# Keys scored between the granules of the gates, values between those of the next head, in a decoder layer for one core

## The chip, the cores and the metric

One core of a Trainium2 chip runs the kernel. The time is that of the device in microseconds (us), the median of several executions. All tensors are float32.

## The reference, cut to what matters

One layer serves a prompt of 256 tokens and 8 sequences of 8 new tokens each (320 tokens together), with 2,048 channels. One projection `h @ w_in` gives everything that the mixer needs. Branch A is a gated linear recurrence (HGRN2) with 8 heads, branch B a differential attention with 8 heads of two softmax maps each; for the 8 sequences it attends to 2,048 past tokens in 16 pages of a shared cache.

```python
u = h @ w_in[l]
hq, hf, hi, hgate, dq, dk, dv, g_hg, g_da = jnp.split(u, IN_SPLIT_POINTS, axis=-1)
# A: chunks of 64 tokens, state S per head
A = jnp.where(causal, einsum('bhncd,bhnsd->bhncs', qg, kg), 0.0)
o = A @ v + qg @ S_prev;  S = exp(G_last) * S_prev + dS
o_hg = rms_norm(o, hg_norm_w[l]) * silu(hgate)
# B: past keys and values are pages of cache_k and cache_v
p = softmax(q @ k.T * DA_DH ** -0.5 + t5_bias)      # two maps
o_da = rms_norm((p[:, 0] - lam * p[:, 1]) @ v, da_subln_w[l]) * (1.0 - lam_init)
mixed = (sigmoid(g_hg) * (o_hg @ w_branch_hg) + sigmoid(g_da) * (o_da @ w_branch_da)) @ w_out
```

A norm, a residual and a SwiGLU feed-forward with 5,632 hidden channels follow. The updated states, the keys and the values are outputs too.

## The kernel before, in words

**Granules.** The unit of dense work is a granule, a 512 KB piece of weights (128 partitions x 1,024) that multiplies two of the 16 channel tiles of the input into four output tiles of 320 columns. For accuracy each weight is split: ScalarE (ACT) copies it to a rounded `w_hi` (`round_hi`, L368, in the opening L352), VectorE (DVE) subtracts for `w_lo` (`split_lo`, L345), and TensorE (PE) makes three matmuls (L386 to L388) for each, 24 in a granule. Eight granules make a set of four tiles in PSUM banks 0 to 3. There are four buffers for the split weights, so a split runs at most four granules ahead of PE. DVE reads a set's banks in `read_set` (L429), and the next set's first granule waits for this, bank by bank.

**Rounds.** After an opening of 7 sets the kernel runs 8 rounds (`pe_round`, `act_round`, `vec_round`, `sync_round`, `pool_round`). A round has two halves. In the gate half PE does the 8 granules of a set of merge gates (A0 to A7 in the order of transfers), and after granule q the products of a head, `pe_head(q)`: attention of the prompt and the chunked recurrence. In the second half PE does the 8 granules of the next head's set (D0 to D7), and between them the paged attention of one sequence (`pe_mix`): four quads of keys (`scores`, 16 matmuls L797 for four pages in groups of 32 columns), the new keys' scores (L803), the sums of squares for the norms (L828), the transposes of the exponentials (`pt`, L835), 16 pages of values (L817) and the transposes back (L851). The last round has no next head and so no D granules.

**ACT and DVE** run each in the order of their program: `act_round` and `vec_round` give for each granule q the split first, then the head's and the mix's steps of that q. ACT reads a quad's scores (`g0` to `g3`, L679), makes the exponential `p` (L710), squares and square roots (`sq`, `rt`, L697 to L704), copies (`q`, L688 and L691; `o`, `o_second`). DVE takes maxima (`m0` to `m3`, L735 and L751) and the norms' reciprocals (L758, L765).

**Transfers.** All 512 KB pieces go through a ring of 12 slots in the order of the list `ROUND`: kind A (gates), K (a page of keys), D (next head), V (a page of values). The sync queue (SP) issues them strictly in this order (L673), and before each waits until the piece that held its slot is used: a weight when DVE has split it, a page of keys when its quad is scored, a page of values when its matmuls are done.

```python
ROUND = (items("A", 0, 8) + items("K", 0, 4) + items("D", 0, 1) + items("K", 4, 8) + items("D", 1, 2)
         + items("K", 8, 12) + items("D", 2, 3) + items("K", 12, 16) + items("D", 3, 6) + items("V", 0, 8)
         + items("D", 6, 7) + items("V", 8, 16) + items("D", 7, 8))
```

GpSimd's queue (POOL) stores the gate set, the new states, and then loads the next head's tiles and old states (`head_loads`, L413 to L421).

**Banks.** Banks 4 to 7 serve the head's products and the paged attention in turn: scores alternate between 4 and 5, the head's output `o` is in 5, its new-state product `ds_s` in 6 and 7. `Steps` are the counters by which the engines wait for each other; a name such as `s0` or `g3` is one step of a round.

Of the kernel before, what the change touches and what calls it, by code (L numbers as in the profile page):

```python
# [19 lines left out]
ALU = mybir.AluOpType  # L20
ACT = mybir.ActivationFunctionType
AX_X = mybir.AxisListType.X
F32 = mybir.dt.float32
# [50 lines left out]
def items(kind, a, b):  # L74
# [40 lines left out]
def build(nc, xT, ck, cv, st, pt, w_in, w_hg, w_da, w_out, w_up, w_dn, nrm, hgw, lbl, lamv,  # L115
          table, c_ident, c_scan, c_causal, c_own, c_hot, c_coef,
          y_T, k_T, v_T, h_p, h_s):
    with ExitStack() as ctx:
# [65 lines left out]
        v_new = sb("v_new", [NQ, HEADS * DV], F32, at_r)  # L184
# [10 lines left out]
        state = sb("state", [P, 4, DV], F32, at_r)  # L195

# [3 lines left out]
        lg = sb("lg", [P, T], F32, at_h)  # L200
# [3 lines left out]
        kd = sb("kd", [P, T], F32, at_h)  # L204
# [4 lines left out]
        i_own = sb("i_own", [CHUNK, NB, DV], F32, at_h)  # L209
# [8 lines left out]
        s_all = sb("s_all", [P, PAST + NQ], F32, at_mix)  # L218
# [218 lines left out]
        def act_head(act, q, h):  # L437
# [6 lines left out]
            if q == 2:  # L444
# [3 lines left out]
                act.wait_ge(h_vec.sem, h_vec.at(h, "fg"))  # L448
# [13 lines left out]
            if q == 4:  # L462
                act.wait_ge(h_pe.sem, h_pe.at(h, "i_t"))
                act.activation(i_tok[:, 0:4, :], ps[0:CHUNK, 6, :].rearrange("p (c d) -> p c d", c=4), ACT.Copy)
                h_act.done(act.activation(i_tok[:, 4, :], ps[0:CHUNK, 7, 0:P], ACT.Copy), "i_tok")
            if q == 6:
                act.wait_ge(h_pe.sem, h_pe.at(h, "kd_t"))
                act.activation(kd_tok[:, 0:4, :], ps[0:CHUNK, 4, :].rearrange("p (c d) -> p c d", c=4), ACT.Copy)
                h_act.done(act.activation(kd_tok[:, 4, :], ps[0:CHUNK, 7, P:2 * P], ACT.Copy), "kd_tok")
# [10 lines left out]
        def vec_head(dve, q, h):  # L480
# [11 lines left out]
            if q == 2:  # L492
# [1176 lines left out]
```

## Time and profile before

| what | value |
|---|---|
| median of 3 executions | 2310.08 us (2309.76 to 2313.56) |
| the profiled execution | 2310.6 us, its span 2309.0 us |
| busy in the span: PE, DVE, ACT | 92%, 45%, 36% |
| mean granted clock of PE | 0.950 |
| moved | 443.86 MB, 192 GB/s on average |
| rounds | from about 210 to 1,090 us |

The profile is of one execution. PE's busy time overstates its work, since matmuls overlap: a matmul of 320 columns lasts 309 ns and the next starts 147 ns after it. A wait in the tables is idle time of an engine just before an instruction, put down to what released it last. The granted clock is the share of TensorE's full speed: 1 is 2.4 GHz, 0.5 is 1.2.

### The profile page before, as it was taken

To read this page: it belongs to the slowest core of one execution; us is meant where nothing else is said; L and a number is where in the kernel's file an instruction comes from. 1 tells how busy PE (TensorE), PEld (TensorE's weight loads), DVE (VectorE), ACT (ScalarE), POOL (GpSimd) and SP (SyncE) were. 2 spreads that over 40 slices of the span, in tenths; PEclk is the share of its full clock that TensorE was granted. 3 is DMA by queue.
4 is the path that set the end of the run, shared out by engine and by line. 5 is a ranking of instruction groups with operands and counts; after the bars stand their busy time and mean duration, and the time that the engine had idled before them with its cause. 6 is when DMAs were issued, how large, how long until landed. Compare 5 with 4: busy or idle time off the path is not lost.

```text
span 2309.0 us, 38951 instructions
## 1 busy us (share of the span) xinstructions
PE 2123.5 (92%) x14722; PEld 1975.9 (86%) x14722; DVE 1050.6 (45%) x1315; ACT 838.8 (36%) x1074; POOL 74.4 (3%) x118
## 2 busy tenths in 40 slices
PE   7999888888888888886999989999999999999995
PEld 7999676767676767673999879999999999999994
DVE  6444343434343425243554464444444444545545
ACT  5224342424242424233434343333333333434432
POOL 1001101010101010100000000000000000000000
PEclk9999998989899989897999989999999999999997
DMA  7766675767666675748564334444444444444431
GB/s 253 158 238 229 243 277 217 273 234 267 245 242 251 229 270 211 287 188 325 169 236 146 127 98 158 149 152 152 147 153 146 148 152 145 147 153 136 160 131 46
DMA packets 123845, 443.86 MB, mean 192 GB/s; under 512 B 14486, under 2 KB 18598, under 8 KB 123729
## 3 DMA queue, kind: packets, MB, share of 16 engines
q1 hardware_dynamic: 113872, 403.78, 49.3%
q0 software_dynamic: 9920, 39.38, 5.9%
q8 instruction: 33, 0.54, 0.1%
q14 instruction: 20, 0.16, 0.0%
HBM read 423.19 MB, written 22.54 MB: 193 GB/s over the span
## 4 chain that ended last, share of the span: by engine, by line
PE 83%; DMA 6%; SPq 3%; DVE 3%; issue 2%; ACT 2%; ACTq 0%; DVEq 0%
PE ps L386 21%; PE ps L387 20%; PE ps L388 20%; DMA raw<-w_in 5%; PE ps L1370 4%; PE ps L1372 4%; PE ps L1371 4%; PE ps L797 3%; SPq L673 2%; SPq L668 1%; PE ps L626 1%; PE ps L817 1%; PE ps L835 1%; DVE w_lo L345 1%; PE ps L613 1%
## 5 line engine op out<-in xcount | busy, mean ns | idle before, releaser
L345 DVE TENSOR_TENSOR w_lo<-raw,w_hi 128x1024 fp32r<-128x1024 f32 x416 | 504.2, 1224 | 698.2 <-ACT w_hi L368 321.3
L386 PE MATMUL ps<-x_hi,w_hi 128*128 128x320 f32 x1408 | 461.0, 327 | 63.1 <-DVE stage L429 36.4
L387 PE MATMUL ps<-x_hi,w_lo 128*128 128x320 f32 x1408 | 448.7, 319 | 0.0
L388 PE MATMUL ps<-x_lo,w_hi 128*128 128x320 f32 x1408 | 447.4, 318 | 0.0
L386 PE MATMUL ps<-h_hi,w_hi 128*128 128x320 f32 x1408 | 436.0, 310 | 11.2 <-DVE h_lo L1310 10.6
L387 PE MATMUL ps<-h_hi,w_lo 128*128 128x320 f32 x1408 | 435.1, 309 | 0.0
L388 PE MATMUL ps<-h_lo,w_hi 128*128 128x320 f32 x1408 | 435.0, 309 | 0.0
L340 ACT ACTIVATE w_hi<-raw 128x1024 fp32r<-128x1024 f32 x240 | 250.4, 1057 | 417.4 <-PE ps L388 417.4
L386 PEld LDWEIGHTS ps<-x_hi,w_hi 128*128 128x128 f32 x1408 | 277.8, 197 | 101.8 <-issue 38.6
L387 PEld LDWEIGHTS ps<-x_hi,w_lo 128*128 128x128 f32 x1408 | 278.2, 198 | 0.0
L388 PEld LDWEIGHTS ps<-x_lo,w_hi 128*128 128x128 f32 x1408 | 277.1, 197 | 0.0
L386 PEld LDWEIGHTS ps<-h_hi,w_hi 128*128 128x128 f32 x1408 | 264.7, 188 | 13.2 <-ACT stage L1246 11.5
L387 PEld LDWEIGHTS ps<-h_hi,w_lo 128*128 128x128 f32 x1408 | 264.7, 188 | 0.2
L388 PEld LDWEIGHTS ps<-h_lo,w_hi 128*128 128x128 f32 x1408 | 264.7, 188 | 0.0
L1370 PE MATMUL ps<-hid_hi,w_hi 128*128 128x320 f32 x704 | 217.3, 309 | 0.0
L1371 PE MATMUL ps<-hid_hi,w_lo 128*128 128x320 f32 x704 | 217.2, 309 | 0.0
L1372 PE MATMUL ps<-hid_lo,w_hi 128*128 128x320 f32 x704 | 217.2, 309 | 0.0
L368 ACT ACTIVATE w_hi<-raw 128x1024 fp32r<-128x1024 f32 x120 | 126.1, 1051 | 229.7 <-DMA raw<-w_in 227.2
L797 PE MATMUL ps<-raw,q_rows 128*32 128x512 f32 x512 | 89.4, 834 | 54.9 <-ACT n_rs L704 49.7
L1370 PEld LDWEIGHTS ps<-hid_hi,w_hi 128*128 128x128 f32 x704 | 132.0, 187 | 0.1
L1371 PEld LDWEIGHTS ps<-hid_hi,w_lo 128*128 128x128 f32 x704 | 132.0, 187 | 0.0
L1372 PEld LDWEIGHTS ps<-hid_lo,w_hi 128*128 128x128 f32 x704 | 132.0, 187 | 0.0
(263 smaller groups left out, 2324.1 us busy)
## 6 DMA issues: line engine op xcount, KB each, us to landing
raw<-w_in SPq DMA_DIRECT2D x176, 512.0 KB, 8.9
raw<-w_up SPq DMA_DIRECT2D x176, 512.0 KB, 3.3
raw<-ck SPq DMA_DIRECT2D x128, 512.0 KB, 5.7
raw<-cv SPq DMA_DIRECT2D x128, 512.0 KB, 6.0
raw<-w_dn SPq DMA_DIRECT2D x88, 512.0 KB, 3.2
raw<-w_out SPq DMA_DIRECT2D x32, 512.0 KB, 4.0
uT<-stage POOLq DMA_DIRECT2D x14, 640.0 KB, 3.7
raw<-w_hg SPq DMA_DIRECT2D x16, 512.0 KB, 5.3
```

Source lines behind the costliest of these rows:

```text
L340: act.activation(w_hi[slot % HALVES][:, :], raw[slot][:, :], ACT.Copy).then_inc(hi_ready, 1)
L345: dve.tensor_tensor(w_lo[half][:, :], raw[slot][:, :], w_hi[half][:, :].bitcast(F32), ALU.subtract).then_inc(lo_ready, 1)
L368: act.activation(w_hi[q % HALVES][:, :], raw[ring_of(r).slot[kind, q]][:, :], ACT.Copy).then_inc(hi_ready, 1)
L386: pe.matmul(out, wh[:, c, m, :], xh(c), start=first, stop=False)
L387: pe.matmul(out, wl[:, c, m, :], xh(c), start=False, stop=False)
L388: mm = pe.matmul(out, wh[:, c, m, :], xl(c), start=False, stop=last)
L613: ins = pe.matmul(ps[:, 6 + k, :], kd_tok[:, 4, :], i_own[:, 4 * k:4 * k + 4, :], start=True, stop=True)
L673: sp.dma_start(raw[slot][:, :], src).then_inc(raw_landed[slot], 16)
L797: ins = pe.matmul(ps[32 * j:32 * j + 32, 4 + g % 2, :], q_rows[:, h, :], raw_all[:, at:at + QUAD, h * PAGE:(h + 1) * PAGE], start=e == 0, ...
L1370: pe.matmul(ps[:, m, 0:T], wh[:, c], xh, **dict(add, start=q == 0))
L1371: pe.matmul(ps[:, m, 0:T], wl[:, c], xh, **add)
L1372: ins = pe.matmul(ps[:, m, 0:T], wh[:, c], xl, **dict(add, stop=q >= 3))
```

## The change

The list of transfers puts a quad of keys behind every two gate pieces, and the values in quads between the last four pieces of the next head; both halves of a round have 24 pieces. The slots of the last round follow the same order. On PE, a quad of keys is scored after gate granules 1, 3, 5 and 7, all in bank 7, each after ACT has read the one before; the new keys' scores come first, after granule 0. Values come in quads after next-head granules 3, 4, 5 and 6; the sums of squares stand before the third quad, in banks 4 and 5. The head's products use three banks, 4 to 6: `i_own` is made in two halves and the new-state product in two parts, the second (`ds_s1`) after next-head granule 0, with DVE's `s_new1` behind it. DVE makes the prompt's masked scores and their maxima in step 1 instead of 2. ACT's copies `q` come first in a round instead of after granule 5; the roots `rt` and DVE's norms come behind the last split. The wait of GpSimd's queue before the load of `v_new` goes, as `v_new` has a place of its own in the second half. Some tiles share memory (`lg` and `kd` are now `fg`).

The diff, cut to its core. New functions `act_pages` and `vec_pages` hold what `act_mix` and `vec_mix` held, by step name instead of q.

```diff
-ROUND = (items("A", 0, 8) + items("K", 0, 4) + items("D", 0, 1) + items("K", 4, 8) + items("D", 1, 2)
-         + items("K", 8, 12) + items("D", 2, 3) + items("K", 12, 16) + items("D", 3, 6) + items("V", 0, 8)
-         + items("D", 6, 7) + items("V", 8, 16) + items("D", 7, 8))
-ROUND_SLOTS = {item: (i + 6) % RING for i, item in enumerate(ROUND)}
-LAST_SLOTS = {item: ROUND_SLOTS[item] for item in items("A", 0, 8)}
-LAST_SLOTS.update({("K", p): ((2, 6, 0, 4)[p // 4] + p % 4) for p in range(16)})
-LAST_SLOTS.update({("V", p): (8 + p) % RING for p in range(16)})
+ROUND = (items("A", 0, 2) + items("K", 0, 4) + items("A", 2, 4) + items("K", 4, 8) + items("A", 4, 6)
+         + items("K", 8, 12) + items("A", 6, 8) + items("K", 12, 16) + items("D", 0, 4) + items("V", 0, 4)
+         + items("D", 4, 5) + items("V", 4, 8) + items("D", 5, 6) + items("V", 8, 12) + items("D", 6, 7)
+         + items("V", 12, 16) + items("D", 7, 8))
+ROUND_SLOTS = {item: i % RING for i, item in enumerate(ROUND)}
+LAST_SLOTS = {item: i % RING for i, item in enumerate(i for i in ROUND if i[0] != "D")}
...
-        h_pe = Steps(sem("h_pe"), "scores vk i_t kd_t a ds pd_t pv ds_s o", 1)
+        h_pe = Steps(sem("h_pe"), "scores vk i_t kd_t a ds pd_t pv ds_s0 o ds_s1", 1)
...
-        h_vec = Steps(sem("h_vec"), "fg kin G Gd s max nmax qkd rc rcl pd2 pd own aT st1 st2 st3 st4 s_new o", 1)
+        h_vec = Steps(sem("h_vec"), "fg kin s max nmax G Gd qkd rc rcl pd2 pd own0 aT st1 st2 st3 st4 own1 s_new0 o s_new1", 1)
...
-        k_pe = Steps(sem("k_pe"), "s0 s1 s2 ss s3", 1)
-        k_act = Steps(sem("k_act"), "q g0 g1 sq g2 rt g3 p silu", 1)
-        k_vec = Steps(sem("k_vec"), "m0 m1 m2 near m3 mx nmx r w rs on rs_da silu da og", 1)
+        k_pe = Steps(sem("k_pe"), "new s0 s1 s2 s3 ss", 1)
+        k_act = Steps(sem("k_act"), "q g0 g1 g2 g3 p sq rt silu", 1)
+        k_vec = Steps(sem("k_vec"), "new m0 m1 m2 near m3 mx nmx r w rs on rs_da silu da og", 1)
...
-                act.wait_ge(h_vec.sem, h_vec.at(h, "fg"))
+                act.wait_ge(h_vec.sem, h_vec.at(h, "kin"))
...
+            def own_part(b):
+                return dve.tensor_tensor(
+                    i_own[:, :, :], i_tok[:, 4:5, :].broadcast_to([CHUNK, NB // 2, DV]),
+                    own[:, 4 * b:4 * b + 4].unsqueeze(2).broadcast_to([CHUNK, NB // 2, DV]), ALU.mult)
+
+            def new_state(b, bank):
+                for k in range(4 * b, 4 * b + 4):
+                    last = SEQ + NQ * k + NQ - 1
+                    ins = dve.scalar_tensor_tensor(s0[:, k, :], s0[:, k, :], eG[:, last:last + 1],
+                                                   ps[:, bank, k % 4 * DV:(k % 4 + 1) * DV], ALU.mult, ALU.add)
+                h_vec.done(ins, f"s_new{b}")
+
             if q == 6:
                 dve.wait_ge(h_act.sem, h_act.at(h, "i_tok"))
-                h_vec.done(dve.tensor_tensor(
-                    i_own[:, :, :], i_tok[:, 4:5, :].broadcast_to([CHUNK, NB, DV]),
-                    own[:, :].unsqueeze(2).broadcast_to([CHUNK, NB, DV]), ALU.mult), "own")
-                dve.wait_ge(h_pe.sem, h_pe.at(h, "a"))
+                h_vec.done(own_part(0), "own0")
+                dve.wait_ge(h_act.sem, h_act.at(h, "kd_tok"))
...
+                dve.wait_ge(h_pe.sem, h_pe.at(h, "ds_s0"))
+                h_vec.done(own_part(1), "own1")
             if q == 9:
                 dve.wait_ge(h_pe.sem, h_pe.at(h, "o"))
-                for b in range(NB):
-                    last = SEQ + NQ * b + NQ - 1
-                    ins = dve.scalar_tensor_tensor(s0[:, b, :], s0[:, b, :], eG[:, last:last + 1],
-                                                   ps[:, 6 + b // 4, b % 4 * DV:(b % 4 + 1) * DV],
-                                                   ALU.mult, ALU.add)
-                h_vec.done(ins, "s_new")
+                new_state(0, 6)
                 h_vec.done(dve.tensor_copy(o_hg[:, bass.ds(h, 1), :].rearrange("p a t -> p (a t)"),
-                                           ps[:, 5, 0:T]), "o")
+                                           ps[:, 4, 0:T]), "o")
+            if q == 10:
+                dve.wait_ge(h_pe.sem, h_pe.at(h, "ds_s1"))
+                new_state(1, 5)
...
+                pe.wait_ge(h_vec.sem, h_vec.at(h, "s"))
+                h_pe.done(five(x[:, 2, :], 6, 4, 3 * P), "i_t")
             if q == 4:
                 pe.wait_ge(h_vec.sem, h_vec.at(h, "qkd"))
                 pe.wait_ge(h_act.sem, h_act.at(h, "i_tok"))
-                h_pe.done(five(kd, 4, P), "kd_t")
+                h_pe.done(five(kd, 4, 5, T), "kd_t")
...
-                for k in range(2):
-                    ins = pe.matmul(ps[:, 6 + k, :], kd_tok[:, 4, :], i_own[:, 4 * k:4 * k + 4, :],
-                                    start=True, stop=True)
-                h_pe.done(ins, "ds_s")
+                h_pe.done(pe.matmul(ps[:, 6, :], kd_tok[:, 4, :], i_own[:, :, :], start=True, stop=True), "ds_s0")
+            if q == 8:
+                pe.wait_ge(h_act.sem, h_act.at(h, "o_att"))
+                pe.wait_ge(h_vec.sem, h_vec.at(h, "own1"))
+                h_pe.done(pe.matmul(ps[:, 5, :], kd_tok[:, 4, :], i_own[:, :, :], start=True, stop=True), "ds_s1")
             if q == 7:
                 pe.wait_ge(h_vec.sem, h_vec.at(h, "st4"))
-                pe.wait_ge(h_act.sem, h_act.at(h, "o_att"))
...
-            pool.wait_ge(h_vec.sem, h_vec.at(h, "s_new"))
+            pool.wait_ge(h_vec.sem, h_vec.at(h, "s_new1"))
...
+            elif what in ("g0", "g1", "g2", "g3"):
+                g = int(what[1])
+                act.wait_ge(k_pe.sem, k_pe.at(r, f"s{g}"))
+                w = 4 * PAGE if g < 3 else 3 * PAGE
+                k_act.done(act.activation(s_all[:, g * 4 * PAGE:g * 4 * PAGE + w], ps[:, 7, 0:w],
+                                          ACT.Identity, bias=far[:, 0:1]), what)
+            elif what == "p":
+                act.wait_ge(k_vec.sem, k_vec.at(r, "nmx"))
+                k_act.done(act.activation(s_all[:, :], s_all[:, :], ACT.Exp, bias=mxk[:, 5:6],
...
+                dve.wait_ge(k_pe.sem, k_pe.at(r, "new"))
+                k_vec.done(dve.tensor_tensor(s_all[:, PAST:], ps[:, 7, 0:NQ], near[:, PAGE:], ALU.add), "new")
...
+            for p in range(QUAD * g, QUAD * g + QUAD):
+                pe.wait_ge(*landed(r, ("K", p)))
+            if g:
+                pe.wait_ge(k_act.sem, k_act.at(r, f"g{g - 1}"))
+            else:
+                pe.wait_ge(k_vec.sem, k_vec.at(r, "new"))
...
+            pe.wait_ge(h_vec.sem, h_vec.last(r))
...
+        def norm_sums(pe, r):
+            pe.wait_ge(k_act.sem, k_act.at(r, "sq"))
+            pe.wait_ge(v_vec.sem, v_vec.at(r, "p1"))
...
         def act_round(act, r):
             full = not isinstance(r, int)
+            act_pages(act, r, "q")
             for q in range(1, 8):
                 round_hi(act, r, "A", q)
                 act_head(act, q, r)
-                if q == 5:
-                    act_mix(act, -1, r)
+                if q in (3, 5, 7):
+                    act_pages(act, r, f"g{q // 2 - 1}")
             for q in range(8):
                 if full:
                     round_hi(act, r, "D", q)
                 if q == 0:
                     act_head(act, 8, r)
-                act_mix(act, q, r)
+                if q == 1:
+                    act_pages(act, r, "g3")
+                if q == 2:
+                    act_pages(act, r, "p")
+                if q == 3:
+                    act_pages(act, r, "sq")
+                if q == 4:
+                    act_pages(act, r, "p0")
+                if q == 5:
+                    act_pages(act, r, "pn")
+            act_pages(act, r, "rt")
+            act_pages(act, r, "silu")
             if full:
                 round_hi(act, r + 1, "A", 0)
-            act_mix(act, 8, r)
+            act_pages(act, r, "o")
 
         def vec_round(dve, r):
             full = not isinstance(r, int)
@@ -875,17 +884,29 @@
                 round_lo(dve, r, "A", q)
                 if q == 1:
                     read_set(dve, hg_set(r), 0, SETS_U + 1)
+                    vec_pages(dve, r, "new")
                 vec_head(dve, q, r)
+                if q == 4:
+                    vec_pages(dve, r, "m0")
+                if q == 6:
+                    vec_pages(dve, r, "m1")
             for q in range(8):
                 if full:
                     round_lo(dve, r, "D", q)
+                if q == 0:
+                    vec_pages(dve, r, "m2")
                 if q == 1:
                     read_set(dve, gate_set(r), 1, SETS_U + 2 + r)
                     vec_head(dve, 9, r)
-                vec_mix(dve, q, r)
+                if q == 2:
+                    vec_head(dve, 10, r)
+                    vec_pages(dve, r, "most")
+                if q == 4:
+                    vec_pages(dve, r, "p1")
+            vec_pages(dve, r, "norm")
             if full:
                 round_lo(dve, r + 1, "A", 0)
-            vec_mix(dve, 8, r)
+            vec_pages(dve, r, "o")
 
         def pe_round(pe, r):
             full = not isinstance(r, int)
@@ -894,17 +915,41 @@
             def granule(s, d, q):
                 in_products(pe, d, q, lambda m: pe.wait_ge(set_out, 4 * s + m - 3))
 
+            def next_head(q):
+                if full:
+                    granule(hg_set(r + 1), at + 8 + q, q)
+
             for q in range(8):
                 granule(gate_set(r), at + q, q)
                 pe_head(pe, q, r)
-            pe_mix(pe, r, lambda q: granule(hg_set(r + 1), at + 8 + q, q) if full else None)
+                if q == 0:
+                    new_scores(pe, r)
+                if q % 2:
+                    scores(pe, r, q // 2)
+            next_head(0)
+            pe_head(pe, 8, r)
+            next_head(1)
+            next_head(2)
+            turn(pe, r)
+            next_head(3)
+            turn_new(pe, r)
+            values(pe, r, 0)
+            next_head(4)
+            values(pe, r, 1)
+            next_head(5)
+            norm_sums(pe, r)
+            values(pe, r, 2)
+            next_head(6)
+            values(pe, r, 3)
+            new_values(pe, r)
+            next_head(7)
+            turn_back(pe, r)
 
         def pool_round(pool, r):
             store_set(pool, gate_set(r), 1, GATE + 4 * r)
             pool_head(pool, r)
             pool.wait_ge(u_stored, 16 * (SETS_U + 1) + 16 * r)
             pool.sem_inc(stage_free, 1)
-            pool.wait_ge(v_pe.sem, v_pe.at(r - 1, "new"))
             pool.dma_start(v_new[:, :], v_rows.rearrange("(b q) h d -> b q (h d)", q=NQ)[
                 bass.ds(r, 1)].rearrange("a q d -> (a q) d")).then_inc(v_n_landed, 16)
             pool.wait_ge(head_stored, HEAD_STORES * (r + 1))
```

## Rows read from the trace of the kernel before

**Rows 1.** The page, section 2: the span in 40 equal slices, GB/s of each

```profile
GB/s 253 158 238 229 243 277 217 273 234 267 245 242 251 229 270 211 287 188 325 169 236 146 127 98 158 149 152 152 147 153 146 148 152 145 147 153 136 160 131 46
```

**Rows 2.** One line's instructions, L579 (the head's first matmul): ns, first and last start

```profile
L579 PE MATMUL ps<-mk,mq x32: 272/322/373, 223.1 to 1001.7; 64*128 64x128 f32 x32
```

**Rows 3.** Stretches of a round: us, busy PE PEld DVE ACT POOL, clock, DMA, GB/s

```profile
566.00:574.00 8.00, 8.00 (x62) 7.70 (x61) 7.89 (x15) 4.83 (x10) 0.00 (x0) 1.00 0.53 182
...
582.00:590.00 8.00, 8.00 (x45) 6.11 (x43) 3.19 (x5) 1.33 (x2) 0.75 (x1) 1.00 0.00 0
590.00:598.00 8.00, 8.00 (x40) 4.87 (x40) 2.56 (x9) 0.69 (x1) 1.46 (x3) 0.59 0.25 90
...
614.00:622.00 8.00, 1.64 (x8) 0.46 (x12) 2.63 (x3) 4.75 (x6) 0.00 (x0) 0.79 1.03 406
622.00:630.00 8.00, 8.00 (x64) 6.69 (x57) 4.31 (x11) 4.91 (x5) 0.00 (x0) 0.78 0.80 277
...
646.00:654.00 8.00, 4.87 (x60) 2.92 (x53) 3.06 (x3) 4.12 (x5) 0.00 (x0) 0.93 1.01 411
654.00:662.00 8.00, 3.76 (x19) 3.51 (x18) 3.77 (x7) 2.56 (x3) 0.00 (x0) 0.86 1.03 410
662.00:670.00 8.00, 7.66 (x43) 7.14 (x44) 3.44 (x7) 3.76 (x5) 0.00 (x0) 0.79 0.77 301
```

**Rows 4.** Waits of the sync queue, 556 to 667 us: total, times, longest

```profile
SPq L673 <- PE ps L797: 21.7, 2, 20.9
```

**Rows 5.** Waits of PE, 556 to 667 us: total, times, longest

```profile
PE ps L797 <- ACT n_rs L704: 6.8, 1, 6.8
PE ps L386 <- DVE stage L429: 4.6, 1, 4.6
PE ps L386 <- DVE w_lo L345: 2.4, 1, 2.4
PE ps L817 <- DMA raw<-cv: 0.7, 1, 0.7
```

**Rows 6.** Timeline of PE, the second quad of keys: start, us, what

```profile
601.33 1.92 PE L797 MATMUL ps<-raw,q_rows 128*32 128x512 f32 x16
```

**Rows 7.** Timeline of ACT in the opening: start, us, what, idle before it

```profile
201.69 1.06 ACT L352 ACTIVATE w_hi<-raw 128x1024 fp32r<-128x1024 f32 x1 [2.46 <-PE ps L388]
```

**Rows 8.** Groups by line, whole span: busy us, mean ns, idle before

```profile
L691 ACT ACTIVATE k_own<-k_all 128x64 f32 (+1 forms) x8 | 2.1, 257 | 0.1
...
L710 ACT ACTIVATE s_all<-s_all,mxk 128x2056 f32<-128x2056 f32 x8 | 16.1, 2015 | 0.3 <-DVE mxk L753 0.2
...
L735 DVE TENSOR_REDUCE mxk<-s_all 128x1 f32<-128x512 f32 x24 | 16.3, 680 | 10.8 <-ACT s_all L679 10.8
...
L758 DVE RECIPROCAL n_rs<-n_rs 128x320 f32<-128x320 f32 x8 | 17.2, 2146 | 0.0
```

**Rows 9.** Timeline of PE, ACT, DVE and PE again, a round's start

```profile
657.38 0.38 PE L851 MATMUL ps<-ident,o_rows 128*128 128x128 f32 x2
...
659.57 1.06 ACT L368 ACTIVATE w_hi<-raw 128x1024 fp32r<-128x1024 f32 x1
...
660.65 1.22 DVE L345 TENSOR_TENSOR w_lo<-raw,w_hi 128x1024 fp32r<-128x1024 f32 x1 [2.24 <-ACT w_hi L368]
...
662.34 0.41 PE L386 MATMUL ps<-x_hi,w_hi 128*128 128x320 f32 x1 [4.57 <-DVE stage L429]
```

**Rows 10.** Timeline of PE, last round: first scores, first branch granule

```profile
1038.38 5.34 PE L797 MATMUL ps<-raw,q_rows 128*32 128x512 f32 x32
...
1088.04 0.61 PE L386 MATMUL ps<-br_hi,w_hi 128*128 128x320 f32 x1 [6.78 <-DVE w_lo L345]
```

**Rows 11.** DMA issues by line: count, KB each, median us to landing

```profile
raw<-w_in SPq DMA_DIRECT2D x176, 512.0 KB, 8.9
raw<-w_up SPq DMA_DIRECT2D x176, 512.0 KB, 3.3
```

More of the change, by code:

```diff
@@ L513, in vec_head @@
                 h_vec.done(dve.tensor_scalar(nmx[:, :], mx[:, :], -1.0, None, ALU.mult), "nmax")
+            if q == 2:
+                dve.wait_ge(h_act.sem, h_act.at(h, "lg"))
+                chain(dve.tensor_tensor_scan(G[:, :], scan_keep[:, :], lg[:, :], 0.0, ALU.mult, ALU.add), "G")
+                for t0, k, n in ((0, SEQ // CHUNK, CHUNK), (SEQ, NB, NQ)):
+                    g = G[:, t0:t0 + k * n].rearrange("p (k n) -> p k n", n=n)
+                    ins = dve.tensor_tensor(lg[:, t0:t0 + k * n].rearrange("p (k n) -> p k n", n=n),
+                                            g[:, :, n - 1:n].broadcast_to([P, k, n]), g, ALU.subtract)
+                h_vec.done(ins, "Gd")
             if q == 4:
@@ L715, in act_mix @@
                     "p (c k) -> p c k", c=8), ACT.Copy), "p0")
+            elif what == "pn":
                 act.wait_ge(v_pe.sem, v_pe.at(r, "pn"))
                 v_act.done(act.activation(p_new[:, :], ps[0:NQ, 7, 0:P], ACT.Copy), "pn")
[L718 to L720 removed]
+            else:
                 act.wait_ge(v_pe.sem, v_pe.at(r, "new"))
@@ new lines, in new_scores, with scores @@
+            pe.wait_ge(k_act.sem, k_act.at(r, "q"))
+            for e in range(2):
+                for j in range(4):
+                    h = 2 * j + e
+                    ins = pe.matmul(ps[32 * j:32 * j + 32, 7, 0:NQ], q_rows[:, h, :], k_own[:, h, :],
+                                    start=e == 0, stop=e == 1)
+            k_pe.done(ins, "new")
+        def scores(pe, r, g):
+            for p in range(QUAD * g, QUAD * g + QUAD):
+                pe.wait_ge(*landed(r, ("K", p)))
+            if g:
+                pe.wait_ge(k_act.sem, k_act.at(r, f"g{g - 1}"))
+            else:
+                pe.wait_ge(k_vec.sem, k_vec.at(r, "new"))
+            at = ring_of(r).slot["K", QUAD * g]
+            for e in range(2):
+                for j in range(4):
+                    h = 2 * j + e
+                    ins = pe.matmul(ps[32 * j:32 * j + 32, 7, :], q_rows[:, h, :],
+                                    raw_all[:, at:at + QUAD, h * PAGE:(h + 1) * PAGE], start=e == 0, stop=e == 1)
+            k_pe.done(ins, f"s{g}")
@@ L837, in pe_mix, with turn_new, values, new_values @@
             v_pe.done(ins, "pt")
-            dense(5)
+        def turn_new(pe, r):
             pe.wait_ge(v_act.sem, v_act.at(r, "p0"))
             v_pe.done(pe.transpose(ps[0:NQ, 7, 0:P], s_all[:, PAST:], ident[:, :]), "pn")
-            values(0, 8)
-            dense(6)
-            values(8, 16)
+        def norm_sums(pe, r):
+            pe.wait_ge(k_act.sem, k_act.at(r, "sq"))
+            pe.wait_ge(v_vec.sem, v_vec.at(r, "p1"))
+            pe.matmul(ps[:, 4, 0:T], ones[:, :], n_rs[:, :], start=True, stop=True)
+            k_pe.done(pe.matmul(ps[:, 5, 0:SEQ], ones[:, :], n_rs2[:, :], start=True, stop=True), "ss")
+        def values(pe, r, g):
+            for p in range(QUAD * g, QUAD * g + QUAD):
+                if p == PAGES // 2:
+                    pe.wait_ge(v_vec.sem, v_vec.at(r, "p1"))
+                if p == PAGES - 1:
+                    pe.wait_ge(v_act.sem, v_act.at(r, "pn"))
+                    pe.wait_ge(v_n_landed, 16 * r + 16)
+                pe.wait_ge(*landed(r, ("V", p)))
+                slot = ring_of(r).slot["V", p]
+                for j in range(4):
+                    ins = pe.matmul(ps[32 * j:32 * j + 32, 6, 0:2 * DV], p_keys[:, p, 32 * j:32 * j + 32],
+                                    raw[slot][:, 2 * DV * j:2 * DV * (j + 1)], start=p == 0, stop=False)
+                ins.then_inc(page_used, 1)
+        def new_values(pe, r):
             for j in range(4):
```

172 lines of the change are left out of this document (48 added, 124 removed).

## The prediction

> **What bounds the kernel now.** I read the page's forty slices first. The kernel falls into an opening, the eight rounds (about 210 to 1,090 us) and a rest in which TensorE (PE) is busy throughout. In the rounds the transfer rate swings between two levels from slice to slice, a slice being about half a round [rows 1]. The change touches only the rounds. The head's first matmul recurs every round, at 223.1 us in the first and 1,001.7 us in the last: (1001.7 - 223.1) / 7 = 111.2 us a round [rows 2]. I take one round, 555.7 to 667.6 us (111.9 us), as the sample.
>
> The stretches of 8 us show why the rate swings [rows 3]. In the gate half PE is busy 8 us of 8 and the transfers run at a fraction (182 GB/s from 566 to 574); from 582 to 590 us they stand still. From 614 to 622 and 646 to 662 us they are saturated, at 406 to 411 GB/s, and PE is busy 1.6 us of 8 in the worst stretch. So the round has enough transfer time, but puts it in the wrong half. A round moves 48 pieces of 524,288 bytes and some 2.5 MB of others (a 640 KB store, 512 KB each of old and new states, the head's tiles), 27.7 MB; at the 410 GB/s of the saturated row that is 68 us of 111. The wait table of the sync queue names the lock: 20.9 us behind the first scores [rows 4]. The ring had filled with pages of keys, and keys were scored only after the eighth gate granule.
>
> PE's waits in the sample come to 6.8 + 4.6 + 2.4 + 0.7 = 14.5 us [rows 5]: 6.8 for the square root, which stands in ScalarE's (ACT's) queue behind a granule whose weights landed late, 2.4 and 0.7 for late pieces themselves, 4.6 for the head's four banks to be read at the round's start. A second loss hides in busy time: the granted clock was 0.59, 0.79, 0.78, 0.93, 0.86 and 0.79 in six stretches [rows 3], that is, part of each at the lower level (1.2 instead of 2.4 GHz). The missing parts times 8 us are (0.41 + 0.21 + 0.22 + 0.07 + 0.14 + 0.21) x 8 = 10.1 us; about 1 of it fell on idle time, so 9 cost something. **Bare work of PE in a round: 111.9 - 14.5 - 9 = 88.4 us.**
>
> **The change, part by part.**
>
> *Quads of keys after gate granules 1, 3, 5 and 7.* The four groups of 16 matmuls (1.92 us at the full clock [rows 6]) only move, so PE's work stays 88.4. Each frees four slots at once, so the sync queue gets room for six pieces per two granules. Six pieces last 6 x 1.28 = 7.7 us at 410 GB/s, and PE needs at least 2 x 3.52 (a granule, from the period of ACT's copies that wait on PE [rows 7]) + 1.9 = 8.9 us for the same part, most often 11 with the head's products. The pieces freed by quad g are those of quad g+2 and two granules. Nothing is late here.
>
> *What the quads wait for.* All scores go through one bank, so quad g+1 waits for ACT to read g (0.67 us). ACT's work between the sigmoid and g0 is about 9 us: a logarithm, exponentials, two copies; by my walk g0 is read 17.4 us after the round's first granule begins and quad 1 is due at 20.5. The head's transposes now wait for VectorE (DVE) to finish `s`, which stands behind `new`, a small addition that waits for the new keys' scores on PE: those end about 2 us after the first head products, the `s` is done some 2.3 us later, within the 3.5 us of gate granule 1. Cost nothing, under that granule; bounded by 0 and, if the cover is missed, 1 us. The maxima m0 and m1 (0.68 us [rows 8]) enter DVE's gate half, where DVE is busy 7.89 us of 8 in one stretch [rows 3]; m0 comes right behind it, and by my walk the split of granule 5 is still done 2.5 us before PE needs it. Under 1 us if not.
>
> *Banks of the head.* Bank 7 leaves the head: the new states' second product waits for `o_att` and the second half of `i_own` and stands after next-head granule 0. The multiply of 1.21 us becomes two. DVE's second `s_new` then starts when that product ends, 4.5 us into the half, and behind it on DVE stand the last maxima and ACT's exponential (2.0 us [rows 8]): done about 10.5 us into the half. The transposes of the weights are due after granule 2, at 3 x 3.52 + 1.0 = 11.6 us. Hidden with a margin of 1 us; if it is missed, at most 1 to 2 us a round. The exponential no longer follows a square root, so its 1.28 us table load goes; it was in no PE wait of the sample and I take nothing for it.
>
> *Order and place of the transfers.* Equal halves (24 pieces each) and use in the order of arrival. In the second half my walk gives: V0 to V7 and D4 have landed by 12 us; V9 waits for D3's split (14 us), V10 for the first value page to be used, at 18.6 us. D6 lands at 24 to 27 and D7 at about 32 us, due on PE at 31 and 37 us with 3 us ahead of them for the two splits. That removes the 6.8, 2.4 and 0.7 us: **-9.9**. The sums of squares now stand after granule 5 and `rt` after granule 7's split, so no quad waits for `rt`.
>
> *Round start.* This wait stays. PE's last transposes (657.38) release ACT, then come a table load, the copy of A1 (659.57), DVE's split (660.65) and the read of bank 0, and PE goes on at 662.34 [rows 9]. The change puts ACT's `q` (three copies of at most 0.26 us [rows 8], 0.76) into this chain, after `o_second` and ahead of A1: 4.6 + 0.76 = **5.4 us**, +0.8.
>
> *Clock.* The drop at 590 us came in the head's products of 8 columns, before any wait, and stays: 3.3 us. The one behind the round-start wait stays: 1.7 us. Those at 618 and 652 us followed waits that go: 9 - 5 = **-4**. That later quads follow granules directly has a precedent at the full clock (601.33 us, 1.92 us [rows 6]).
>
> *Seams.* Values in four groups instead of two add two changes of operands: +0.5.
>
> Sum of a round: 88.4 + 5.4 + 5.0 + 0.5 = 99.3 us against 111.2, so **-11.9 us; seven rounds -83 us.**
>
> *Last round* (no next head, so nothing covers the chain). Before: 1088.04 - 1038.38 = 49.7 us from the first scores to the branch weights [rows 10]. Three quads (5.6 us) and the new scores (0.5) move ahead of that point. What is left: quad 3 3.5, product 1.0, DVE's states and maxima to 6.8, exponential to 9.0, transposes at the lower clock 3.7 to 12.9, copy and turn 1.4, values 9.4, sums of squares 1.9, new value 0.6: 26.3; but DVE's norm (two reciprocals, the longer 2.15 us [rows 8], and four products, 5.9 us in all) now stands after `rt`, which ends at 23.2, and its gated output at 29.1 starts the 6.6 us to the first branch granule: 35.7. So 49.7 - 35.7 - 6.1 = **-7.9**; I take -7.
>
> **Total: -83 - 7 = -90 us.** The profiled execution took 2310.6 us (span 2309.0), 0.5 above the median of 2310.08, so both give 2220 us.
>
> **A rule against it.** The heads' loads and state stores go out from GpSimd, in the sample at 597 to 607 us, ahead of the value pages. The wait for the last round's `new` before `v_new` goes (it was long past). All of it now stands behind `s_new1`, and the loads fall some 15 to 25 us into the half, where value pages and D6 are on the way. The landing times show shared bandwidth: 8.9 us for w_in in the rounds, 3.3 for equal pieces of w_up [rows 11]. The loads are 1.3 MB, 3 us at 410 GB/s, as much as my margin. The Trainium skill, DMA: Bandwidth & Descriptors, section Issuing engines are not separate DMA queues, says the transfers of all issuing engines interleave on the same 16. By it the loads are no free extra lane and D6 or D7 could slip; the trace agrees in kind.
>
> **The rivals.**
> 1. *Forecast* (0.66): 2220, own range 2204 to 2238 (each round 97 to 101.9 us).
> 2. *Late next-head weights or ACT/DVE order* (0.20): D6/D7 slip, the exponential or the round start is missed, 3 to 6 us a round with the clock drop behind it: 2240 to 2262.
> 3. *Better* (0.07): fewer clock drops, round 95 us: 2190.
> 4. *Slower than before* (0.05): the mechanism is the quad as a gate. If quad 0 or 1 waits for four pieces that only the previous quad released, PE stops in the gate half where it never did: 6 x 1.28 + about 2 us of first landing = 9.7 us against 8.9 of cover, plus the queue of the head's loads. It decides from 3 us per quad, 12 us a round; then the time passes 2310, to some 2320. Against it stands that releases are two quads ahead.
> 5. *Nothing moves* (0.02): the transfers are the bound whatever the order. 68 us in 99 speaks against it.
>
> **How the numbers follow.** 2220 is case 1. The range 2196 to 2256 takes in case 1, most of 2, half of 3; 2 in 10 stay out. A measurement of this kernel tells 0.2% (4.6 us) from no change. Faster 0.93 (cases 1 to 3), same 0.02, slower 0.05.
>
> **What would show it.** First matmul of the head every 99 us; transfers without a standstill in the gate half and without saturated stretches of 16 us; PE waits of a round: one of 5.4 us at the stage read with the longer chain, nothing at the square root; two clock drops, one at the head's 8-column products, one behind the round start; last value to branch weights with DVE's norm as releaser. Wrong would be waits before `i_t`, before the transposes for the exponential, or before granules 6 and 7 for weights.

## The result and the profile after

The changed kernel takes 2211.92 us (median of 4 executions, 2210.85 to 2212.78) against 2311.82 us for the kernel before: a ratio of 0.9564, 95% interval 0.9549 to 0.9579, or 99.9 us less. The forecast was 90 us less, 2220 us, within 2196 to 2256. The profiled execution took 2210.85 us, its span is 2209.3.

The page of the kernel after (sections 1 and 2): the clock and the transfer rate of the rounds, now to slice 18, are those to set beside [rows 1].

```profile
PE 2094.8 (95%) x14722; PEld 1951.7 (88%) x14722; DVE 1047.0 (47%) x1323; ACT 828.0 (37%) x1066; POOL 74.1 (3%) x118
PEclk9999999999999999979999899999999999999997
GB/s 258 159 232 266 254 292 268 305 285 277 314 225 318 249 286 275 306 260 186 243 154 144 77 149 147 151 151 144 150 151 144 145 146 145 162 149 139 159 123 48
```

The rate of the rounds is higher, but no more even than before: 225 to 318 GB/s in slices 5 to 17, where [rows 1] have 211 to 287. The head's first matmul gives the pace of a round, as in [rows 2]:

```profile
L587 PE MATMUL ps<-mk,mq x32: 272/322/373, 222.4 to 911.9; 64*128 64x128 f32 x32
```

(911.9 - 222.4) / 7 = **98.5 us a round**, before 111.2: seven rounds give 89 us. The opening ends 0.7 us sooner, and the stretch from the last head's first matmul to the first branch granule is 988.37 - 911.9 = 76.5 us long and was 86.3 [rows 2, 10], 9.9 less unrounded. The sum is 99.7. Everything behind the branch's start takes 1220.9 us in both.

Stretches of one round after (us, busy PE PEld DVE ACT POOL, clock, DMA, GB/s), to be read against [rows 3]:

```profile
517.00:525.00 8.00, 8.00 (x75) 5.82 (x74) 6.39 (x17) 4.98 (x7) 0.00 (x0) 1.00 0.00 0
525.00:533.00 8.00, 8.00 (x62) 6.79 (x60) 4.49 (x12) 5.46 (x15) 0.00 (x0) 1.00 0.83 273
533.00:541.00 8.00, 8.00 (x64) 7.28 (x57) 5.19 (x8) 3.45 (x5) 0.00 (x0) 1.00 0.97 340
541.00:549.00 8.00, 8.00 (x59) 6.08 (x58) 1.96 (x5) 2.13 (x3) 0.00 (x0) 1.00 0.70 268
549.00:557.00 8.00, 8.00 (x49) 6.59 (x47) 5.14 (x8) 1.33 (x2) 0.03 (x1) 1.00 0.83 299
557.00:565.00 8.00, 8.00 (x51) 5.24 (x51) 2.30 (x6) 1.53 (x2) 0.73 (x1) 0.79 0.37 123
565.00:573.00 8.00, 8.00 (x51) 7.05 (x50) 2.78 (x9) 2.82 (x3) 1.95 (x3) 1.00 0.94 325
...
589.00:597.00 8.00, 8.00 (x72) 6.58 (x71) 1.23 (x1) 1.23 (x2) 0.00 (x0) 1.00 1.03 410
597.00:605.00 8.00, 7.36 (x73) 5.58 (x71) 5.94 (x5) 6.49 (x10) 0.00 (x0) 1.00 1.03 410
605.00:613.00 8.00, 3.40 (x13) 3.40 (x14) 4.97 (x9) 5.55 (x8) 0.00 (x0) 0.66 1.01 403
```

The gate half runs from 511.1 to 562.5 us. Two of the forecast's signs did not come. There is still a standstill in it (517 to 525 us, as 582 to 590 us in [rows 3]), and the saturated stretches before the next round last 24 us, where the forecast wanted none of 16. What moved is the mean: the gate half carries 225 GB/s (before, from 550.5 to the first quad at 593.6 us, 131), the second half 345 (before 323). PE is whole in every stretch but those around the round's start, although the last 24 us are saturated: most of the pieces that land there are for the next round. The table of PE's waits for 517 to 615 us has one row where [rows 5] have four:

```profile
PE ps L385 <- DVE stage L428: 5.2, 1, 5.2
```

and that of the sync queue for the same stretch waits for the scores (L801) in four pieces, the longest 12.5 us, where [rows 4] have one of 20.9. It waits longer for them in all (33.9 us against 21.7), but no wait of PE comes of it. L835 are the values:

```profile
SPq L682 <- PE ps L801: 33.9, 4, 12.5
SPq L682 <- PE ps L835: 8.6, 4, 5.4
```

What is left of waiting is the chain at the round's start, with the copies `q` (L691, L694) now inside it; compare [rows 9]. Timeline of the changed kernel, in columns of start, length, engine, line, work and, in brackets, the idle time before it with what ended it:

```profile
603.98 0.38 PE L848 MATMUL ps<-ident,o_rows 128*128 128x128 f32 x2
...
604.86 1.28 ACT L691 ACT_TABLE_LOAD   x1 [0.24 <-issue]
606.15 0.52 ACT L691 ACTIVATE q_rows<-q_all 64x64 f32 x2
606.68 0.26 ACT L694 ACTIVATE k_own<-k_all 128x64 f32 x1
606.85 1.04 ACT L367 ACTIVATE w_hi<-raw 128x1024 fp32r<-128x1024 f32 x1
...
607.92 1.23 DVE L344 TENSOR_TENSOR w_lo<-raw,w_hi 128x1024 fp32r<-128x1024 f32 x1 [0.75 <-ACT w_hi L367]
...
609.60 0.63 PE L385 MATMUL ps<-x_hi,w_hi 128*128 128x320 f32 x1 [5.24 <-DVE stage L428]
```

### The profile page after: what moved, and what is told of

Same layout as the page of the kernel before. It is cut to its first block, busy times and chain, and to the rows that moved or that the text cites. A ratio compares the mean times of both kernels' runs of the same rounds, so it can differ in the third digit from the quotient of the medians.

```text
span 2209.3 us, 38997 instructions
## 1 busy us (share of the span) xinstructions
PE 2094.8 (95%) x14722; PEld 1951.7 (88%) x14722; DVE 1047.0 (47%) x1323; ACT 828.0 (37%) x1066; POOL 74.1 (3%) x118
## 4 chain that ended last, share of the span: by engine, by line
PE 92%; DVE 3%; ACT 2%; DMA 2%; issue 1%; SPq 0%; ACTq 0%; DVEq 0%
PE ps L385 23%; PE ps L386 22%; PE ps L387 22%; PE ps L1417 5%; PE ps L1415 5%; PE ps L1416 5%; PE ps L801 3%; PE ps L835 2%; DMA raw<-w_in 1%; PE ps L635 1%; PE ps L810 1%; PE ps L629 0%; PE ps L631 0%; PE ps L578 0%; PE ps L608 0%
## 5 line engine op out<-in xcount | busy, mean ns | idle before, releaser
L385 PE MATMUL ps<-x_hi,w_hi 128*128 128x320 f32 x1408 | 455.4, 323 | 51.3 <-DVE stage L428 41.5
L386 PE MATMUL ps<-x_hi,w_lo 128*128 128x320 f32 x1408 | 442.4, 314 | 0.0
L387 PE MATMUL ps<-x_lo,w_hi 128*128 128x320 f32 x1408 | 441.8, 314 | 0.0
L385 PEld LDWEIGHTS ps<-x_hi,w_hi 128*128 128x128 f32 x1408 | 272.0, 193 | 108.8 <-issue 61.6
L386 PEld LDWEIGHTS ps<-x_hi,w_lo 128*128 128x128 f32 x1408 | 272.3, 193 | 0.0
L387 PEld LDWEIGHTS ps<-x_lo,w_hi 128*128 128x128 f32 x1408 | 271.3, 193 | 0.0
L1367 DVE TENSOR_TENSOR hid_lo<-hidden,hid_hi 128x320 fp32r<-128x320 f32 x88 | 43.3, 492 | 154.8 <-ACT w_hi L1306 154.4
```

The lines of the kernel that those rows point to most:

```text
L385: pe.matmul(out, wh[:, c, m, :], xh(c), start=first, stop=False)
L386: pe.matmul(out, wl[:, c, m, :], xh(c), start=False, stop=False)
L387: mm = pe.matmul(out, wh[:, c, m, :], xl(c), start=False, stop=last)
L1367: dve.tensor_tensor(hid_lo[slot % HALVES][:, :], hidden[:, bass.ds(k, 1), :].rearrange("p a t -> p (a t)"), hid_hi[slot % HALVES][:, :].bi ...
```

## The experiments

All ratios are to runs of the kernel before on the same chip (2310.9 to 2312.8 us). The pace of a round is worked out as above. Where a pace is split into waits, clock and bare work, the figures are means of its seven rounds: the waits are PE's idle times, the clock's share is half of the time at the lower level while PE was not idle, and the bare work is the rest. Before, this gives 14.3 + 8.8 + 88.1 = 111.2 us; in the changed kernel 5.2 + 3.7 + 89.6 = 98.5.

**Half the bytes of keys and values, before and after.**

```diff
-                sp.dma_start(raw[slot][:, :], src).then_inc(raw_landed[slot], 16)
+                n = 512 if kind in "KV" else 1024
+                sp.dma_start(raw[slot][:, 0:n], src[:, 0:n]).then_inc(raw_landed[slot], 16)
```

(In the changed kernel the first use of the four slots that no weight has filled is loaded whole.)

> The kernel before, with only the first half of each page of keys and values loaded (256 KB instead of 512, the rest of the slot is stale, so the attention of the sequences is wrong). Order, waits and all work of the engines stay. Theory (the gain came from transfers that now run in the gate half): with 8.4 MB less a round the bursts behind the lock are a third shorter, the waits for the square root and for late pieces (9.9 of 14.5 us in the sample) shrink to under 3, the clock drops behind them go too: about 100 us a round, 2225 to 2245 us. Rival (the gain came from the shorter order of steps on ScalarE, VectorE and PE): the waits stay, above 2290 us.

Measured: 2265.89 us, ratio 0.9806 (0.979 to 0.9823), 105.0 us a round. This lies in neither theory's range: 45 us less, where 66 to 86 were expected. The table of PE's waits, whole span:

```profile
PE ps L386 <- DVE w_lo L345: 33.1, 10, 9.2
PE ps L798 <- ACT n_rs L705: 25.9, 8, 4.7
```

and that of the sync queue, 550 to 662 us:

```profile
SPq L674 <- PE ps L798: 22.3, 3, 20.3
```

The root's wait fell to 25.9 us in all (49.7 before), but the queue still stood 20.3 us behind the scores: fewer bytes shorten the burst behind the lock, they do not open the lock.

> The changed kernel with the same half pages. Theory (transfers no longer hold PE up anywhere but for 0.2 us in some rounds and 1 us in the last): 2205 to 2212 us, no more than 0.3% faster than the changed kernel, waits of PE in a round only the 5.2 us at its start. Rival (transfers still bound part of it): 2190 us or less.

Measured: 2210.88 us, ratio 0.9568 (0.9552 to 0.9584), 98.7 us a round: the changed kernel's time to 1 us. Some 30% of a round's bytes taken out (8.4 of 27.7 MB) gives nothing that can be told from the spread. The bytes of keys and values are no bound of it any more.

**Two groups of values again.**

```diff
-         + items("K", 8, 12) + items("A", 6, 8) + items("K", 12, 16) + items("D", 0, 4) + items("V", 0, 4)
-         + items("D", 4, 5) + items("V", 4, 8) + items("D", 5, 6) + items("V", 8, 12) + items("D", 6, 7)
-         + items("V", 12, 16) + items("D", 7, 8))
+         + items("K", 8, 12) + items("A", 6, 8) + items("K", 12, 16) + items("D", 0, 6) + items("V", 0, 8)
+         + items("D", 6, 7) + items("V", 8, 16) + items("D", 7, 8))
...
-            values(pe, r, 0)
             next_head(4)
-            values(pe, r, 1)
             next_head(5)
             norm_sums(pe, r)
+            values(pe, r, 0)
+            values(pe, r, 1)
+            next_head(6)
             values(pe, r, 2)
-            next_head(6)
```

> The changed kernel with one part undone: values in two groups of eight pages, after next-head granules 5 and 6, and their transfers in the same order (D0 to D5, V0 to V7, D6, V8 to V15, D7); both halves still have 24 pieces. Theory (order of use inside the half matters, since V11 can only be loaded when V0 is used, now 10 us later): V15 and D7 land late, PE waits 1 to 2 us a round before granule 7 or the next one, less 0.4 us for two seams: 2218 to 2232 us. Rival (only the equal halves matter): 2209 us, same as the changed kernel or 3 us faster.

Measured: 2242.25 us, ratio 0.9698 (0.9682 to 0.9715), 102.5 us a round, 4.0 more than the changed kernel. That is above the theory's range of 2218 to 2232. The mechanism is the forecast one (timelines of the sync queue and of PE): the sync queue's eight value pages took from 588.40 to 607.51 us, and D7, issued behind them, was late.

```profile
588.40 19.11 SPq L681 DMA_DIRECT2D raw<-cv  x8
607.70 2.10 SPq L681 DMA_DIRECT2D raw<-w_in  x3
```

```profile
612.87 0.64 PE L834 MATMUL ps<-raw,p_keys 128*32 128x256 f32 x8 [0.36 <-DMA raw<-cv]
...
616.49 0.42 PE L384 MATMUL ps<-x_hi,w_hi 128*128 128x320 f32 x1 [2.41 <-DVE w_lo L343]
```

The waits are 2.8 us a round more than in the changed kernel and the clock costs 1.7 more, while the bare work, with two seams fewer, is 0.6 less: together the 4.0. I had counted the wait (and less of it, 1 to 2 us) and not the clock drop behind it. The last round, 4.4 us longer, gives the rest. So equal halves alone are not enough.

**A megabyte more a round.**

```diff
+            for j in range(2):
+                pool.dma_start(spare[bass.ds(r, 1), j].rearrange("a p n -> (a p) n"),
+                               w_in[0, j]).then_inc(spared, 16)
```

> The changed kernel with 1 MB of useless copies a round within the main memory, issued from GpSimd's queue behind the load of v_new, about 10 us into the second half. It measures the margin that the split of granules 6 and 7 has (about 1.5 and 1.2 us in the profile). Theory: 2.6 us of transfer time fall on D6 and D7, PE waits 1 to 2 us before each of the rounds' last granules, 2218 to 2230 us. Rival (the transfers have room): within 0.2% of the changed kernel.

Measured: 2214.77 us, ratio 0.9581 (0.9565 to 0.9597), 2.9 us more than the changed kernel and within 0.2% of it. The waits for DVE's splits are those of the changed kernel (20.9 us in the whole span, 20.7 there). The rival held. ACT's idle time before the copy of D6 is no longer than it was (of this kernel, then of the changed one):

```profile
594.54 1.06 ACT L369 ACTIVATE w_hi<-raw 128x1024 fp32r<-128x1024 f32 x1 [9.68 <-DMA raw<-w_in]
```

```profile
590.43 1.06 ACT L367 ACTIVATE w_hi<-raw 128x1024 fp32r<-128x1024 f32 x1 [9.84 <-DMA raw<-w_in]
```

A megabyte in front did not make ACT wait longer for D6. But the run did not load D6's own transfer: the copies were issued at 575.8 and 576.4 us and had landed 8.4 us later at most, while the sync queue issued D6 only at 586.9. They ran beside value pages. So the run shows that the stretch before D6 has room. It does not show what a megabyte beside D6 or D7 would cost. That D6's landing is set by the use of the value pages ahead of it in the ring, not by the rate, fits this and was not tried by itself.

**The round's start: copies `q` out of the chain.**

```diff
             full = not isinstance(r, int)
-            act_pages(act, r, "q")
...
             act_pages(act, r, "silu")
+            if full:
+                act_pages(act, r + 1, "q")
```

> The changed kernel with ScalarE's three small copies q made at the end of the round before (behind silu, ahead of the split of A0), not first in the round. Theory: they stand in the chain that ends PE's wait at the round's start, so this wait goes from 5.24 to 4.5 us in seven rounds, 2205 to 2209 us (5 us less). Rival (the copies were hidden): no difference.

Measured: 2209.19 us (2206.73 to 2211.31), ratio 0.9559 (0.9543 to 0.9575), 98.2 us a round. The wait at the start went as forecast: the row of all eight had 41.5 us in the changed kernel and has 37.0, so (37.0 - 5.8) / 7 = 4.5 us each, 0.6 less (5.8 us is one wait before the rounds). In the time it is 2.7 us, too little to be told from the spread.

```profile
PE ps L385 <- DVE stage L428: 37.0, 8, 5.8
```

**Sums, roots and norm earlier; then the bank read earlier; then `q` too.**

```diff
-            act_pages(act, r, "rt")
-            act_pages(act, r, "silu")
+                    act_pages(act, r, "rt")
+                    act_pages(act, r, "silu")
...
-            vec_pages(dve, r, "norm")
+                if q == 5:
+                    vec_pages(dve, r, "norm")
...
             values(pe, r, 0)
+            norm_sums(pe, r)
             next_head(4)
             values(pe, r, 1)
             next_head(5)
-            norm_sums(pe, r)
```

> The changed kernel with the sums of squares two next-head granules earlier (after the first four value pages), the roots and silu on ScalarE and the norm on VectorE in step 5, where both sit idle for 10 us, instead of after the last split. Theory: in the rounds the norm was hidden under next-head granule 7, and PE's order has no gap, so same within 0.1% (2210 to 2214 us), with a few tenths from the last round. Rival (the late norm holds the next round's first split): 4 us or more less.

Measured: 2209.75 us, ratio 0.956 (0.9544 to 0.9576): 2 us less than the changed kernel, 98.6 us a round. The late norm was hidden. The next edit comes on top of this one:

```diff
                 if q == 1:
-                    read_set(dve, hg_set(r), 0, SETS_U + 1)
...
                 round_lo(dve, r + 1, "A", 0)
+                read_set(dve, hg_set(r + 1), 0, SETS_U + 1)
             vec_pages(dve, r, "o")
```

> As norm_early, and VectorE reads the head's four banks (the step that PE's first gate granule waits for) before it waits for the transposed output of the sequence, not behind the split of A1 in the next round. Theory: the chain of 5.24 us (output back, table load, q, split of A1, bank read) no longer ends the wait, PE waits under 0.5 us at the round's start, and the clock drop behind it (6.8 us at the lower level, about 1 of it on idle time) goes: -5.1 and -2.4 us in seven rounds, 2155 to 2172 us. Rival (the split of A1 is needed 3.5 us later anyway and takes the wait over): PE waits 2 to 4 us before granule 1, 2190 us or more.

Measured: 2167.90 us, ratio 0.9376 (0.936 to 0.9392), 92.3 us a round. PE's waits in the seven rounds come to 0.2 us in all, none of them for A1, so the rival did not come. DVE reads each bank as its last matmul ends and PE goes from the transposes back straight into the next gate granule (DVE, then PE):

```profile
586.43 0.49 DVE L428 TENSOR_TENSOR stage<-ps,rs_all 128x320 f32<-128x320 f32 x1 [1.07 <-PE ps L387]
```

```profile
588.88 0.38 PE L848 MATMUL ps<-ident,o_rows 128*128 128x128 f32 x2
589.02 0.40 PE L385 MATMUL ps<-x_hi,w_hi 128*128 128x320 f32 x1
```

The clock drop behind the old wait is gone too; one in the middle of each round is left. A round loses 5.0 us of waits and 1.3 of clock against norm_early, and the kernel 42 us, for the place of one step.

> norm_read and q_early together, q in step 5. Theory: the split of A1 is done 0.2 us before PE needs it in norm_read, so taking 0.8 us out of its chain gives nothing but margin: same as norm_read within 0.2%. Rival (A1 is late there): 3 to 6 us faster than norm_read.

Measured: 2164.67 us, ratio 0.9357 (0.9338 to 0.9376); on another chip 2165.48 us, ratio 0.9382 (0.936 to 0.9404). It is 3.2 us below norm_read, 0.15%: within the theory's 0.2% and within the rival's 3 to 6 us, so the time does not tell them apart. The waits do: norm_read had none for A1 to take away. This version beats both kernels, 46 to 47 us below the changed one.

**ScalarE's order in the kernel before.**

```diff
             if q == 2:
                 group(1)
...
-            if q == 3:
                 group(2)
                 act.wait_ge(k_pe.sem, k_pe.at(r, "ss"))
```

> The kernel before with one line out: g2 and the square roots rt stand on ScalarE ahead of the split of D3, not behind it. It separates ScalarE's order from the transfers. In the trace the split of D3 begins at 616.4 us when its weights land, rt ends at 620.2 and PE's fourth quad starts at 620.4; the sums of squares were ready at about 613.5. Rival (order on ScalarE was the larger part of the loss): rt is done at 615.7, quad 3 starts 4.7 us earlier, and all value pages behind it too: 33 us or more less, 2275 to 2280 us. Theory (the ring's lock is): quad 3 moves, but PE then waits for D3's own weights, and the late pieces behind it take part of the gain back: 10 to 25 us less, 2287 to 2302 us.

Measured: 2283.84 us, ratio 0.9892 (0.9867 to 0.9916), 107.3 us a round: 27 us less, between the two ranges. The fourth quad and granule D3 behind it, timeline of PE:

```profile
604.68 1.92 PE L796 MATMUL ps<-raw,q_rows 128*32 128x512 f32 x16 [1.07 <-ACT n_rs L703]
608.74 0.54 PE L386 MATMUL ps<-x_hi,w_hi 128*128 128x320 f32 x1 [2.03 <-DVE w_lo L345]
```

Of the root's wait, 6.8 us in [rows 5], 1.1 is left, and 2.0 come back as a wait for D3's own weights.

> The kernel before with half pages and with rt ahead of the split of D3, both together. Half pages alone gave 45 us. If half pages and order are separate causes, their gains add up; with transfers at half size what is left of the square root's wait (3.6 us in the round looked at) goes whole: 25 to 30 us below light_before, 2236 to 2242 us. If they are one cause seen twice, it is at most 10 us below light_before. The changed kernel's 2211 should not be reached, since the quads of keys still wait for the end of the gate half.

Measured: 2237.75 us, ratio 0.9689 (0.9665 to 0.9713), 101.9 us a round: 28 us below light_before. The two gains, 27 and 45, add up to the 73 measured. By the expectation's own rule they are two causes.

**The clock drop in the middle of a round.**

```diff
+                if q == 7:
+                    scores(pe, r, 3)
                 pe_head(pe, q, r)
...
-                if q % 2:
+                if q % 2 and q < 7:
```

> The fastest version so far (2164.7 us) with quad 3 of the keys before the head's last products instead of behind them. The clock drops once a round where those products (8 to 64 columns) and quad 3 stand together, 3.4 or 6.8 us at the lower level. Theory (the drop is set off by the narrow products, not by the quad): it stays, and now falls on dense granule D0 in place of quad 3, which costs the same half of its length: within 0.2% of 2164.7. Rival (it needs both in this order): the drops go, 10 to 15 us less.

> The fastest version once more, on the same chip as best_s3, to compare the two: 2160 to 2168 us by every theory.

Measured on one chip: 2163.65 us (ratio 0.9374, 0.935 to 0.9398) and 2165.48 us. No difference, and drops stay (55 and 51 us at the lower level in the eight rounds). So quad 3 behind the products is not what sets them off. What does was not found.

## Why the prediction was right, point by point

**Bound and lock.** Right in the main. The waits of 6.8, 2.4 and 0.7 us are gone from the sample, and light_after shows that the bytes of keys and values cost the changed kernel no time. The picture of an even rate was wrong: the round shown still has a standstill and 24 saturated microseconds, and no wait of PE comes of either. And the step that gave all 9.9 us to "order and place of the transfers" joined two causes. The runs give, per round: 111.2; 107.3 with the root ahead of D3's split; 105.0 with half the bytes; 101.9 with both; 98.5 for the change. The order on ScalarE, which the change also made, is worth 3.9 us by itself. Half the bytes, in the old order, are worth 6.2. The 3.4 us between both together and the change are waits (2.4) and clock (2.4) that neither removes, less 1.4 of bare work that the change adds.

**Bare work.** Forecast 88.4 + 0.5 for seams. The round 516.7 to 615.5 has 98.7 - 5.2 (wait) - 4.1 (clock: missing parts of 0.21, 0.34 and 0.09 times 8 us are 5.1, of which 1.0 fell on idle time) = 89.4 us. Right to 0.5 us. norm_read, nearly without a wait, confirms it: 92.3 us less 2.9 of clock. Over seven rounds, though, the bare work rose from 88.1 to 89.6 us, three times the 0.5 of the seams. That term came from no row; values_two, with two seams fewer, has 0.6 us less, which bears it out. Where the rest of the rise, about 1 us, comes from stays open.

**Round start.** Forecast 5.4 us, measured 5.24; `q` in it forecast 0.76, measured 0.6 with q_early.

**Clock.** Forecast 5.0 us a round, measured 4.1. The places were right, the sizes the wrong way round: of the drops in after, the one at the head's last products is short (3.4 us at the lower level, 1.7 lost) and the one at the round's start long (6.8, of which 2 on idle time, 2.4 lost). Over seven rounds the terms of the sum are 89.6 + 5.2 + 3.7 = 98.5 us, against 88.9 + 5.4 + 5.0 = 99.3: the clock 1.3 and the wait 0.2 too dear, the bare work 0.7 too cheap. That the errors partly cancel is luck. The difference, 0.8 x 7 = 6 us, is the larger part of the 10 missing.

**Hidden steps.** In the seven rounds no wait appeared before `i_t`, before the transposes of the exponentials or at the quads. The exponential: forecast done 10.5 us into the half, and 562.54 to 572.1 is 9.6. D6 was forecast at 24 to 27 us and D7 at 32; their splits began 27.9 and 34.3 us in (590.43 and 596.83), and PE took them at 31.7 and 37.8. So D7 had 1.2 us to spare here, and in two other rounds it was late by 0.2. The rule that issuing engines are no separate queues (the Trainium skill, DMA: Bandwidth & Descriptors, section Issuing engines are not separate DMA queues) gave rival 2 its chance. The trace agrees that the transfers run side by side: from 575 to 590 us it has 2.70 MB from the sync queue's and 1.73 MB from GpSimd's, and D6, issued at 582.7, is among them. No wait of PE came of it in this round, and 1 MB more from GpSimd's queue cost 2.9 us in eight rounds. That does not test the rule against D6 and D7, since those copies had landed before D6 was issued. What made D7 late in values_two was the order of pieces and steps, with no byte added.

**Last round.** Forecast -7 (worked out -7.9), measured -9.9. The chain was right to the transposes (exponential forecast 9.0 us after quad 3 began, measured 965.1 - 955.96 = 9.1; transposes 12.9, measured 12.9). From quad 3 to the first branch granule it took 32.4 us, forecast 35.7. The work moved ahead of quad 3 took 7.4 us (955.96 - 911.9, less 1038.38 - 1001.7), forecast 6.1, which gives part of this back. What failed is the step that let DVE's norm set the branch's start at 29.1 us. Values ran faster than my 9.4 us (8.7 with their waits), the root ended at 19.9 and not 23.2, and the gated output was done 25.6 us in, before the last output of the values (26.1), which set it (timelines of PE and DVE):

```profile
955.96 3.47 PE L801 MATMUL ps<-raw,q_rows 128*32 128x512 f32 x16
...
965.15 3.68 PE L810 MATMUL ps<-ident,s_all 128*128 128x128 f32 x16 [4.66 <-ACT s_all L703]
...
981.11 0.49 DVE L770 TENSOR_TENSOR o_all<-o_all,n_e 128x320 f32<-128x320 f32 x1
981.87 0.22 DVE L773 TENSOR_TENSOR o_all<-o_second,ps 128x64 f32<-128x64 f32 x1 [0.28 <-ACT o_second L729]
...
988.37 0.60 PE L385 MATMUL ps<-br_hi,w_hi 128*128 128x320 f32 x1 [6.78 <-DVE w_lo L344]
```

**The rivals.** 2 did not come, though its place is real: values_two reaches it by order alone (2242 us, in its range). 3 came in part: the clock cost less than forecast, but a round took 98.5 us and not 95. 4 did not come: no quad waited for keys. 5 is refuted by the result, and by light_after.

## What to carry to other kernels

A ring that loads strictly in order and frees in order of use is a schedule: write the order of transfers in the order of use, a few pieces at a time, and spread the consumers over the whole round, since the first consumer that stands late holds everything behind it. Half the bytes gave 45 us; a new order of transfers and steps with all the bytes gave 100. Then look at what the last wait's chain holds that does not belong to it: here a bank read that needed only PE's last matmul stood behind an output and a split of the next piece, and moving it was worth 42 us, with the norm moved out of its way beforehand.

## What was not expected of the hardware

Waits bring clock losses with them that come on top: in values_two, 2.8 us more of waits a round came with 1.7 us more lost to the clock; in norm_read, 5.0 us of waits taken away took 1.3 us of clock loss along (98.6 to 92.3 us a round); from the kernel before to the changed one it was 9.1 us of waits and 5.1 of clock. A megabyte of copies within the main memory a round, in a half where most stretches already carry 286 to 410 GB/s, changed the time by 0.13%; its transfers ran beside value pages and were over before D6 was issued.
